# A Strassen-type MLP on one core: where the last combination is written, and where the shared part is spread in the last block

## What is computed

```
def sq_relu_mlp(xn, w1, w2):
    h = jax.nn.relu(jnp.einsum('btd,df->btf', xn, w1))
    return jnp.einsum('btf,fd->btd', h * h, w2)
...
        xp = xp + sq_relu_mlp(rmsnorm(xp, norm_mlp[layer]), mlp_w1[layer], mlp_w2[layer])
```

## Time and profile before

| what | value |
|---|---|
| median of 3 runs | 2674.62 us (2672.04 to 2677.25) |
| the profiled execution, its own time | 2675.46 us |
| its span, first to last instruction | 2673.7 us |
| PE busy | 2557.2 us, 96% of the span |
| DVE, ACT, POOL busy | 57%, 39%, 45% |
| mean granted TensorE clock | 0.972 |

### The profile page before, as it was taken

The page is one execution under the profiler, slowest core; times in us unless marked ns, Lnnn a source line. Parts: engine busy times, 40 slices in busy tenths (PEclk is TensorE's granted clock), DMA queues, the critical chain, the costliest instruction groups (busy, mean ns, idle before and its releaser), DMA issues.

```text
span 2673.7 us, 44745 instructions
## 1 busy us (share of the span) xinstructions
PE 2557.2 (96%) x16728; PEld 2373.3 (89%) x16728; DVE 1523.8 (57%) x2510; ACT 1043.6 (39%) x1876; POOL 1212.4 (45%) x824
## 2 busy tenths in 40 slices
PE   7999999889879999999999979998999999999997
PEld 6668788766659999999999979998999999999997
DVE  5369886336555555545554587565355545554556
ACT  5348884766532322232223343435222233223322
POOL 4114441017335565556555663323455456545653
PEclk9989999989889999999999989999999999999999
DMA  4402222734461111111111102233111111111112
GB/s 148 137 20 69 86 85 75 230 96 119 140 226 55 41 55 47 39 47 55 47 39 47 47 24 80 76 113 138 44 38 56 39 47 47 55 39 45 49 47 84
DMA packets 109204, 198.73 MB, mean 74 GB/s; under 512 B 22709, under 2 KB 62773, under 8 KB 108805
## 3 DMA queue, kind: packets, MB, share of 16 engines
q1 hardware_dynamic: 104602, 191.85, 23.0%
q10 hardware_dynamic: 4480, 5.27, 0.6%
HBM read 170.97 MB, written 47.17 MB: 82 GB/s over the span
## 4 chain that ended last, share of the span: by engine, by line
PE 66%; DVE 3%; issue 1%; ACT 1%; POOL 0%; DMA 0%; DVEq 0%; ACTq 0%
PE d_ps L2283 40%; PE d_ps L2808 24%; PE d_ps L3170 1%; PE d_ps L2298 1%; DVE xg_low L2309 0%; DVE rstd_all L2370 0%; DVE x_t L2903 0%; DVE x_t L2912 0%; DVE xg_low L3298 0%; POOL m_hidden_low L2652 0%; DVE m_shared_part L2903 0%; DVE m_hidden L2856 0%; PE d_ps L2343 0%; DVE unit_high L2266 0%; POOL unit_low L2270 0%
## 5 line engine op out<-in xcount | busy, mean ns | idle before, releaser
L2283 PE MATMUL d_ps<-xg_high,unit_high 128*128 128x364 f32 (+1 forms) x2112 | 472.5, 332 | 8.3 <-DVE xg_low L3298 3.1
L2283 PE MATMUL d_ps<-xg_high,unit_low 128*128 128x364 f32 (+1 forms) x2112 | 464.7, 328 | 0.0
L2283 PE MATMUL d_ps<-xg_low,unit_high 128*128 128x364 f32 (+1 forms) x2112 | 464.6, 328 | 0.0
L2270 POOL TENSOR_TENSOR unit_low<-unit_raw,unit_high 128x1024 fp32r<-128x1024 f32 x96 | 232.6, 2423 | 400.7 <-DVE unit_high L2266 231.4
L2808 PE MATMUL d_ps<-m_hidden_high,unit_high 128*128 128x272 f32 x1792 | 376.7, 292 | 26.7 <-DVE x_t L2903 14.7
L2283 PEld LDWEIGHTS d_ps<-xg_high,unit_high 128*128 128x128 f32 x2112 | 365.5, 188 | 14.8 <-issue 5.6
L2808 PE MATMUL d_ps<-m_hidden_high,unit_low 128*128 128x272 f32 x1792 | 373.4, 290 | 0.0
L2808 PE MATMUL d_ps<-m_hidden_low,unit_high 128*128 128x272 f32 x1792 | 372.7, 289 | 0.0
L2283 PEld LDWEIGHTS d_ps<-xg_high,unit_low 128*128 128x128 f32 x2112 | 366.9, 189 | 0.0
L2283 PEld LDWEIGHTS d_ps<-xg_low,unit_high 128*128 128x128 f32 x2112 | 365.2, 188 | 0.0
L2659 POOL TENSOR_TENSOR unit_low<-unit_raw,unit_high 128x512 fp32r<-128x512 f32 x128 | 177.8, 1389 | 399.9 <-ACT unit_high L2727 399.9
(11 more groups left out here) (388 smaller groups left out, 3997.5 us busy)
## 6 DMA issues: line engine op xcount, KB each, us to landing
unit_raw<-w_units SPq DMA_DIRECT2D x160, 512.0 KB, 3.7
unit_raw<-w_in SPq DMA_DIRECT2D x48, 256.0 KB, 2.9
proj_rows<-rows SPq DMA_DIRECT2D x32, 256.0 KB, 2.0
s_win<-win_cache SPq DMA_DIRECT2D x2, 3968.0 KB
proj_rows<-rows SPq DMA_DIRECT2D x36, 128.0 KB, 1.8
sw_rows<-proj_rows SPq DMA_DIRECT2D x12, 384.0 KB, 4.7
select_work<-xt SPq DMA_DIRECT2D x8, 546.0 KB, 3.8
x_t<-xt SPq DMA_DIRECT2D x4, 1092.0 KB, 13.5
```

What stands on the lines that cost most here:

```text
L2270: self.nc.gpsimd.tensor_tensor(self.wl[slot][:, :], self.raw[:, slot, :], self.wh[slot][:, :].bitcast(F32), ALU.subtract).then_inc(self.w_ ...
L2283: last = self.nc.tensor.matmul(ps[:, c, 0:USED[c]], w[wslot][:, wk], v[:, k, c, 0:USED[c]], start=(k == 0 and n == 0), stop=(k == nk - 1 a ...
```

## The change

Three things, all inside `stage_mlp`:

1. The fourth combination (`combine(pair, 3)`) is written to `t1` instead of `hidden(1, 0)`. It no longer overwrites operand 4, so it waits only for operand 2's low half (`h_low` 7 * pair + 2 instead of + 5). In exchange the next pair's first combination, which writes `t1` too, waits until all seven low halves are made. This holds in all 8 blocks of both layers.
2. In the last block, `share(m)` for m = 0, 1, 2 comes behind the pair's last addition instead of behind a1; for m = 3 it stays behind a1. The readers of x (ACT's `next_rows`, SP's output DMAs) now also wait for it.
3. In layer 0's last block `next_low` for rows 2m-2, 2m-1 comes in pair m+1 instead of in pair m: none in pair 1, two each in pairs 2 and 3, four after the last addition instead of two.

```
-        SOURCES = {..., 4: hidden(1, 0), 5: hidden(1, 1), 6: hidden(1, 0)}
+        SOURCES = {..., 4: hidden(1, 0), 5: hidden(1, 1), 6: t1}
...
             if y is not None:
                 for o in range(KD):
                     sp.wait_ge(added, ADDED_0 + NPROD * (PAIRS * LAST + o // 2) + 6 + o % 2)
+                    sp.wait_ge(spread, o + 1)
...
             def next_rows(m):
                 for o in (2 * m, 2 * m + 1):
                     act.wait_ge(added, ADDED_0 + NPROD * (PAIRS * LAST + m) + 6 + o % 2)
+                    act.wait_ge(spread, 2 * m + 1 + o % 2)
...
-                    dve.wait_ge(h_low, NPROD * pair - (3 if t == 0 else 0))
+                    dve.wait_ge(h_low, NPROD * pair - (3 if t == 0 else 1))
...
                 if x == 0:
-                        dve.wait_ge(h_low, NPROD * pair - 5)
+                        dve.wait_ge(h_low, NPROD * pair)
                     ins = nc.vector.tensor_tensor(t1, hidden(0, 1), hidden(0, 0), ALU.subtract)
...
                     dve.wait_ge(combined, 4 * pair + 3)
-                    dve.wait_ge(h_low, NPROD * pair + 5)
-                    ins = nc.vector.tensor_tensor(hidden(1, 0), hidden(1, 0), hidden(0, 0), ALU.subtract)
+                    dve.wait_ge(h_low, NPROD * pair + 2)
+                    ins = nc.vector.tensor_tensor(t1, hidden(1, 0), hidden(0, 0), ALU.subtract)
...
-                dve.wait_ge(added, ADDED_0 + NPROD * n + (4 if m == 0 else 2))
+                dve.wait_ge(added, ADDED_0 + NPROD * n + (2 if m == PAIRS - 1 else NPROD))
...
-                        if last and x == 1:
+                        if last and x == (1 if m == PAIRS - 1 else NPROD - 1):
                             share(m)
                         if ahead and j < 4:
                             weigh(*ahead, j)
-                        if last and y is None and m and x in (3, 5):
-                            next_low(2 * m - (2 if x == 3 else 1))
+                        if last and y is None and m >= 2 and x in (3, 5):
+                            next_low(2 * (m - 2) + x // 5)
...
                 if last and y is None:
-                    for o in (KD - 2, KD - 1):
+                    for o in range(KD - 4, KD):
                         next_low(o)
```

More of the change, by code:

```diff
@@ L2587, in chunks @@
             return flat.rearrange("p (c n) -> p c n", c=2)
-        SOURCES = {0: hidden(0, 0), 1: hidden(0, 0), 2: t1, 3: hidden(0, 1), 4: hidden(1, 0), 5: hidden(1, 1), 6: hidden(1, 0)}
+        SOURCES = {0: hidden(0, 0), 1: hidden(0, 0), 2: t1, 3: hidden(0, 1), 4: hidden(1, 0), 5: hidden(1, 1), 6: t1}
         FIRST_PARTS = ((0, 0), (1, 0), (2, 0), (3, 0), (0, 1), (2, 1), (4, 0), (3, 1), (5, 0), (1, 1), (4, 1), (6, 0), (5, 1), (6, 1))
```

## The result

The changed kernel took 2653.76 us (median of 4 runs, 2649.25 to 2657.65) and the kernel before, on the same chip, 2673.33 us (median of 4, 2669.94 to 2677.25). The ratio is 0.9927, 95% interval [0.9910, 0.9944]: the change saves 15 to 24 us. I had predicted 2662.5 with a range from 2656 to 2670. The direction was right and the size, 12 us, too small. The profiled execution of the changed kernel took 2657.65 us, with a span of 2655.9 us.

A forecast was written before the change was run, and what follows sets the result against it. PE works 96% of the span, so only its waits and half clock can yield time. 8.5 + 8.1 + 3.1 - 2.0 + 1.3 - 1.0 - 2.3 - 1.0 - 1.2 - 1.4 = 12.1 us: 2662.5, range 2656 to 2670.

The forecast's parts named there:

- layer 1, pairs 0 and 1: Layer 1's last block: pair 1 starts 8.1 us earlier and runs at full clock, less 1.0 for a new half clock.
- hand-over: Layer 0 into the recurrent block: two more low parts behind the last addition delay DVE, -1.2 us, bounds 0 and 5.8.
- Both waits: Last blocks, pairs 0 and 1: PE waits 5.97 us on a0 through POOL's low halves, then for a4 behind the spread.
- Layer 0, pairs 1 to 3: Layer 0's last block: +1.3 us for a4 freed in pair 1, -1.0 in pair 2, -2.3 and -1.0 in pair 3.
- With more waits I add half of one more stretch at half clock: Layer 0's last block, pair 3: more PE waits bring more half clock, booked at -1.0 us.
- the new half clock in pair 0: Last blocks, pair 0: the new 2.2 us wait may drop PE's clock, 1.0 us for each layer, bounds 0 and 1.7.
- Layer 1's -1.4: Layer 1's last block, pair 3: two spreads ahead of a2 make PE wait at product 5, -1.4 us.
- The gain comes whole: Last blocks: PE keeps full clock, DVE precedes POOL, pairs 2 and 3 lose nothing: 21 us, 2654; chance 0.14.
- No change: Layer 0's pair 0: PE stays held by POOL's halves, if POOL, not DVE, released (4,0); no separate chance given.
- Given back in layer 0: Blocked spreads and low parts, half clock after each wait and a late third tile leave 4.3 us, 2670.3; chance 0.19.
- the wait only moves to POOL: Every block: first combination stands until POOL's seventh low half, costing 18 us, 2680; slower by combination or hand-over 0.05.

The follow-up runs named there:

- one part alone: Two runs against the kernel before: only the fourth combination in t1 (2663.35 us, 0.9961), and only the spread behind the last addition for pairs 0 to 2 (2664.23 us, 0.9966).
- changed, third: The changed kernel measured and traced a third time, nothing altered: 2654.21 us against 2671.34 for the kernel before (0.9932).
- no_row_sums: The changed kernel without POOL's row sums of rows 3 to 7 behind layer 0's MLP, only the counter raised: one run, 2651.67 us.
- low_parts_back: The changed kernel with the next layer's low parts where they stood before, two behind the last addition: 2659.05 us, 0.9956 of the kernel before.
- six_low_and_layer1: The changed kernel with six low parts behind layer 0's last addition; in layer 1, pair 3's spread behind a3 and output issued early: 2653.68 us, 0.9925.

## Why the prediction was right in direction and too small

The sum of 12.1 us against the means of the traces (for layer 0 the four with its code unchanged, for layer 1 the three of the changed kernel), stage by stage (us; the sum is that of the unrounded values):

| term | predicted | measured |
|---|---|---|
| layer 0, pair 0, with the new half clock | 8.5 - 1.0 | 8.5 |
| layer 0, pair 1: a4 freed, full clock | 1.3 + 1.6 | 2.7 |
| layer 0, pair 2 | -1.0 | +0.2 |
| layer 0, pair 3 to the opening | -2.3 - 1.0 | -1.5 |
| hand-over | -1.2 | -0.9 |
| layer 1, pairs 0 and 1 | 8.1 + 1.5 - 1.0 | 8.8 |
| layer 1, pair 3 to the end | -1.4 | -0.5 |
| sum | 12.1 | 17.4 |

**Right.** Both waits had the causes that I named, shown by one part alone for each. The gain ahead of pair 2 was sized within 1 us in each layer (11.3 for 10.4, 8.8 for 8.6). Without a fall of the clock pair 1 starts at 13.4 us, where I had 1544.03 - 1530.13 = 13.9; POOL's chain was 0.34 us quicker than my count of its blocks. What released pair 1 there was, as predicted, POOL's first weights' part, behind a short wait (weight loads, "changed, third"):

```profile
1543.97 0.30 PEld L2810 LDWEIGHTS d_ps<-m_hidden_high,unit_high 128*128 128x128 f32 x2 [0.35 <-POOL unit_low L2660]
```

Layer 1's wait at product 5 of pair 3 was forecast at 1.4 and measured at 1.27. No wait for an addition appears in the other 14 blocks, although DVE and POOL are each busy some 22 us longer there.

**The step that failed** is "Layer 0, pairs 1 to 3". For pairs 2 and 3 I booked -1.0 - 2.3 - 1.0 = -4.3 us, and they cost 1.3, so 3.0 of the missing 5.3 us are here: 1.2 in pair 2, 0.8 in pair 3 and 1.0 in the half clock that I added. Three counts were too dark:
- In pair 2 I let both instructions of pair 1's spread be blocked, to 4.6 us behind the pair's first product. They took 0.73 and 2.39 us, to 4.0, as in this row pair of the changed kernel's DVE timeline; pair 2 starts at 1551.68. The additions behind them made PE wait 1.46 and 1.45 us, less than the 1.58 and 1.47 before, and a3 was not late at all.

```profile
1552.63 0.73 DVE L2913 TENSOR_TENSOR x_t<-x_t,m_shared_part 128x544 f32<-128x544 f32 x1
1553.28 2.39 DVE L2914 TENSOR_TENSOR x_t<-x_t,m_shared_part 128x1088 f32<-128x1088 f32 x1
```

- In pair 3 I counted delays of 1.5 and 5.3 us; PE waited 0.87 and 4.75. In delays, counted as in the prediction, that is 1.1 and 5.0 us, 6.1 against 4.6 before: 1.5 us where I had 2.3. The mechanism was right: a2 is late, and 3.0 of its 4.75 us of wait are blocking by row sums (no_row_sums).
- "With more waits I add half of one more stretch at half clock": from pair 3's product 5 to the opening it is 6.7 us before and after. Products 5 and 6 of pair 3 ran at half clock behind a wait of 4.36 us before and run so behind 4.75 us now. And what DVE does beside them is hidden by just that slowness.

**Sized wrong in the same direction:** the new half clock in pair 0. It cost 1.0 to 1.4 us where it came, near the 1.0 that I had put, but it came in only one of the four traces of layer 0 (pair 1 at 14.60 against 13.4), and in all three of layer 1. Where it came, PE and not POOL's chain set the start of pair 1, against what I had argued. Layer 1's -1.4 was a wait of PE ahead of an end that PE didn't set: the last addition did end later against pair 3's start, by 1.5 us, but it had had 1.0 us to spare before the output transfers' end, and the end moved only by the 0.5 us by which the first transfer left later. I had read the earlier trace rows for PE's wait and put SP's waits at nothing, since they concern rows 0 to 5; that they hold the issue of all eight transfers back until 13.1 us ahead of the end I never asked.

**The hand-over** was right as mechanism, DVE late to the recurrent block and PE's third tile waiting, and the size is near by luck: the waits are 0, 0.39, 0.39 and 1.57 us, 0.6 on the mean, and the rest of the 0.9 is the half clock behind the opening in the first trace. Its bounds, 0 to 5.8, hold all kernels seen.

**The rivals.** "The gain comes whole" gave the time, 2654, but not by its reasons: DVE did not get in ahead of POOL (POOL was first by 0.02 us), in layer 1 PE lost clock behind the short wait, and pairs 2 and 3 did lose, 1.3 us. "No change" falls with the rows: a0 released (4,0), after 2.12 us. "Given back in layer 0" did not happen, nor did "the wait only moves to POOL": the first combination's stricter wait never reached PE. A local gain of 17.4 us on 2673.3 gives 2655.9, just below the lower end of my range; the 2 us from there to the measured 2653.76 are within its interval. The range was too narrow for terms of loss that came out too dark together: pair 2, pair 3, the added half clock and layer 1's end make 3.9 us, layer 0's new half clock half of the rest.

Some things stay open. low_parts_back gained 16 us locally, which is outside the 12 (8 to 15) of its runs, and six_low_and_layer1 16 against 20 (17 to 24); one trace each does not show how often the clock fell in the other runs. And DVE first instead of POOL in the near tie of pair 0 was not tried.

## What to carry to other kernels

Book a loss behind a gain only with a row that shows what binds there: a wait on PE that stands next to an engine's slack, a half-clock stretch or a full DMA queue may already be paid for, as here. When a queue is relieved (DVE in pair 3), ask what it will wait for next; moving work out of it brings nothing once that is the other engine. And before an end is priced, find out whether compute or the output transfers set it.

## What the runs showed of the hardware

- The same 544-element addition of two SBUF operands took 0.73 us beside an idle POOL and 1.37, 1.82 or 2.64 us beside a working one; 1088 elements took 1.28 alone and up to 3.58. Over the whole kernel the change added 26 us of DVE and 27 us of POOL busy time, some 22 us of each outside the last blocks, where PE still has no wait for an addition.
- Eight output transfers issued within 9.9 us ran at 406 GB/s with a DMA share of 1.0 in the rows above, whereas spread over 29 us they stayed at 121 and 224 GB/s in the last two stretches.
- Behind the same wait of 2.12 us in layer 0's pair 0 the changed kernel kept full clock in two of three traces (pair 1 at 13.40 and 13.37) and not in the other (14.60). Over the ten kernels and repeats with parts 1 and 2 of the change, a stretch at half clock followed this wait in three traces in layer 0 and in nine in layer 1; only low_parts_back kept full clock in layer 1 (pair 2 at 24.04, against 25.14 to 25.47).
